# Softmax weights in ten chunks per head instead of twelve, and the pair gate and sums moved to GpSimd

## The reference

```python
def block(i):                       # 128 queries
    ...
    score = jnp.where(causal[None], score, -jnp.inf)
    _, sel = lax.top_k(score, topk)              # 256 keys
    logits = jnp.einsum('bqhd,bqkhd->bqhk', q_b, k_sel) * att_scale
    p = jax.nn.softmax(logits, axis=-1)
    return jnp.einsum('bqhk,bqkhd->bqhd', p, v_sel)
...
y_attn = group_rmsnorm(y_attn, gn_attn, N_HEADS) * jax.nn.silu(az)   # per head of 64
y = jnp.concatenate([y_conv, y_attn], axis=-1) @ w_out
return x + gate[:, None, :] * y
```

## Time and profile before

| | us |
|---|---|
| median of 3 runs | 722.95 (721.53 to 723.73) |
| the profiled execution's own time | 727.4 |
| its span, first to last instruction | 725.2 |
| PE busy | 673.8 (93%) |
| DVE busy | 468.8 (65%) |
| ACT busy | 372.0 (51%) |
| POOL busy | 220.4 (30%) |

### The profile page before, as it was taken

The page is one execution under the profiler, slowest core; times in us unless marked ns, Lnnn a source line. Parts: engine busy times, 40 slices in busy tenths (PEclk is TensorE's granted clock), DMA queues, the critical chain, the costliest instruction groups (busy, mean ns, idle before and its releaser), DMA issues.

```text
span 725.2 us, 8966 instructions
## 1 busy us (share of the span) xinstructions
PE 673.8 (93%) x3219; PEld 556.9 (77%) x3219; DVE 468.8 (65%) x772; ACT 372.0 (51%) x559; POOL 220.4 (30%) x109
## 2 busy tenths in 40 slices
PE   0889997999999999999999999998998999899996
...
GB/s 316 306 257 1 89 165 167 94 178 106 89 87 88 59 49 39 59 29 59 58 30 30 106 213 70 18 174 140 267 117 112 93 118 1 59 85 61 174 116 58
DMA packets 27910, 78.63 MB, mean 108 GB/s; under 512 B 3986, under 2 KB 8410, under 8 KB 27868
## 3 DMA queue, kind: packets, MB, share of 16 engines
...
q10 hardware_dynamic: 344, 1.05, 0.6%
...
## 4 chain that ended last, share of the span: by engine, by line
PE 77%; DVE 9%; ACT 4%; issue 4%; DMA 3%; SPq 2%; ACTq 1%; DVEq 0%
PE ps L726 15%; PE ps L728 15%; PE ps L727 15%; PE ps L906 4%; PE ps L907 4%; PE ps L908 4%; PE ps L844 4%; PE ps L784 2%; PE ps L785 2%; DMA iqs<-hlL 2%; PE ps L765 2%; PE ps L766 2%; DVE acc L1328 2%; DVE phL L1535 2%; PE ps L858 1%
## 5 line engine op out<-in xcount | busy, mean ns | idle before, releaser
L726 PE MATMUL ps<-hH,wH 128*128 128x512 f32 (+1 forms) x544 | 212.5, 391 | 1.5 <-issue 1.4
L728 PE MATMUL ps<-hH,wL 128*128 128x512 f32 (+1 forms) x544 | 211.0, 388 | 0.0
L727 PE MATMUL ps<-hL,wH 128*128 128x512 f32 (+1 forms) x544 | 211.0, 388 | 0.0
L1687 POOL TENSOR_TENSOR wL<-raw,wH 128x1024 fp32r<-128x1024 f32 x35 | 85.7, 2448 | 188.4 <-ACT wH L959 188.4
L726 PEld LDWEIGHTS ps<-hH,wH 128*128 128x128 f32 x544 | 102.6, 189 | 21.8 <-issue 3.2
L728 PEld LDWEIGHTS ps<-hH,wL 128*128 128x128 f32 x544 | 102.6, 189 | 20.5
L727 PEld LDWEIGHTS ps<-hL,wH 128*128 128x128 f32 x544 | 102.7, 189 | 18.4
L1527 DVE CUSTOM_DVE_ANT_0 ps<-ps,bias 128x128 f32<-128x128 f32 (+3 forms) x64 | 48.7, 761 | 45.7 <-PE ps L766 43.7
L1535 DVE TENSOR_TENSOR phL<-ps,phH 128x512 fp32r<-128x512 f32 (+1 forms) x96 | 52.6, 554 | 23.0 <-ACT phH L1164 17.4
L1144 ACT ACTIVATE relu<-ps,wabs 128x384 f32<-128x384 f32 (+5 forms) x48 | 40.2, 848 | 45.1 <-PE ps L785 24.6
L1421 DVE SCALAR_TENSOR_TENSOR score<-relu,wsgn,score 128x384 f32<-128x384 f32 (+5 forms) x42 | 49.7, 1184 | 19.2 <-ACT relu L1144 16.7
...
## 6 DMA issues: line engine op xcount, KB each, us to landing
raw<-in_w_units SPq DMA_DIRECT2D x36, 512.0 KB, 3.3
...
xin<-in_x SPq DMA_DIRECT2D x8, 512.0 KB, 7.9
wa<-in_w_ada SPq DMA_DIRECT2D x8, 512.0 KB, 11.8
...
gw<-in_w_ada SPq DMA_DIRECT2D x8, 512.0 KB, 3.7
...
wo<-in_w_out SPq DMA_DIRECT2D x8, 512.0 KB, 9.3
```

The costliest lines, as they stand in the source:

```text
L726: pe.matmul(out, wH[slot(n)][:, kt, :], hH[:, kt, cols], start=(kt == 0), stop=False)
L727: pe.matmul(out, wH[slot(n)][:, kt, :], hL[:, kt, cols], start=False, stop=False)
L728: mm = pe.matmul(out, wL[slot(n)][:, kt, :], hH[:, kt, cols], start=False, stop=(kt == KT - 1))
L1687: g.tensor_tensor(wL[slot(n)][:], raw[slot(n)][:], wH[slot(n)][:].bitcast(F32), ALU.subtract).then_inc(s_wL, 1)
```

## The change

**Chunks.** The chunks are now lists of key blocks. In half 0 the chunks of block 1 (384 columns) and block 3 (128) become one of 512 columns, (1, 3), block 3 in the free first 128 columns of the bank; in half 1 the same is done with blocks 5 and 7. A head has 3 + 7 = 10 chunks, of which eight are 512 columns wide and two 256. PE transposes and multiplies as much as before; `split_prob` and `low_prob` are 10 each instead of 12. The order within a half changes to 0, (1, 3), 2 and 0 to 4, (5, 7), 6. All tables are written anew for 20 half steps per head.

**Pair gate and sums.** `pair_gate` is now a product of `ya` and `azs` on POOL, and the gain goes into `pair_scale` on DVE at the end. As POOL has the sum not at hand in PSUM, ACT first copies it into `azs` (`keep_sums`, at x = 10 and 14), and POOL adds `dden` in place (`pair_add`). `keep_sums` waits for the sum (`s_yss`) and for POOL's gate product (`s_ygP`), since it writes over `azs`. PE's logits that reuse the banks now wait for `keep_sums` (`s_sums`) instead of `pair_add`. The last pair stays on DVE (`last_gate`, `last_add`, `last_scale`).

**Semaphores.** To make room for the new ones, the loads of the first two tiles of x share a semaphore (the first square waits for both), and so do two pairs of the loads of the last part of `w_ada`.

```diff
@@ -161,26 +161,26 @@
 NPH = 3
 PV_LAG = 2
 
-STEPS = 12
-LOGITS_AT = (4, 11, 13, 16, 18, 21, 23, 26)
-MAX_AT = (6, 11, 14, 16, 17, 22, 23, 25)
-EXP_AT = (10, 14, 17, 17, 22, 24, 27, 30)
+CHUNKS = ([(0,)] + [(1, 3)] + [(2,)], [(j,) for j in range(5)] + [(5, 7)] + [(6,)])
+STEPS = len(CHUNKS[0]) + len(CHUNKS[1])
+LOGITS_AT = (4, 9, 11, 14, 16, 18, 19, 22)
+MAX_AT = (5, 9, 12, 14, 15, 19, 19, 21)
+EXP_AT = (8, 12, 15, 15, 19, 20, 22, 24)
 FIRST_LOGITS = {2: 0, 3: 1, 4: 2, 5: 3, 6: 4, 10: 5, 12: 6, 14: 7}
 TMP_AT, OUT_AT = 4, 5
 LAST = 2 * STEPS * (NH - 1)
 
-DSQ_AT = {24 * (2 * t + 1) + (9 if t < NT - 1 else 7): t for t in range(NT)}
-DENS_AT = {24 * (2 * t + 1) + (11 if t < NT - 1 else 9): t for t in range(NT)}
-KEEP_AT = {24 * (2 * t + 1) + (13 if t < NT - 1 else 11): t for t in range(NT)}
-SUMS_AT = {24 * (2 * t + 2) + 11 + 4 * half: (t, half) for t in range(NT - 1) for half in range(2)}
-SUMS_AT[LAST + 17] = (NT - 1, 0)
-GATE_AT = {24 * (2 * t + 2) + 12: t for t in range(NT - 1)}
-ADD_AT = {24 * (2 * t + 2) + 13 + 4 * half: (t, half) for t in range(NT - 1) for half in range(2)}
-ADD_AT[LAST + 19] = (NT - 1, 0)
-OUT_HIGH_AT = {24 * (2 + ct) + 15: ct for ct in range(4)}
-OUT_HIGH_AT.update({LAST + x: 4 + n for n, x in enumerate((13, 16, 20, 22))})
-OUT_LOW_AT = {LAST + x: 4 + n for n, x in enumerate((15, 18, 22))}
-EARLY_PARTS = {4: 2, 5: 2, 6: 2, 7: 3, 8: 3, 10: 2, 11: 2}
+HEAD = 2 * STEPS
+DSQ_AT = {HEAD * (2 * t + 1) + (7 if t < NT - 1 else 5): t for t in range(NT)}
+DENS_AT = {HEAD * (2 * t + 1) + (11 if t < NT - 1 else 7): t for t in range(NT)}
+KEEP_AT = {HEAD * (2 * t + 1) + (13 if t < NT - 1 else 9): t for t in range(NT)}
+SUMS_AT = {HEAD * (2 * t + 2) + 9 + 4 * half: (t, half) for t in range(NT - 1) for half in range(2)}
+SUMS_AT[LAST + 15] = (NT - 1, 0)
+KEEP_SUMS_AT = {HEAD * (2 * t + 2) + 10 + 4 * half: (t, half) for t in range(NT - 1) for half in range(2)}
+OUT_HIGH_AT = {HEAD * (2 + ct) + 12: ct for ct in range(4)}
+OUT_HIGH_AT.update({LAST + x: 4 + n for n, x in enumerate((11, 14, 17, 18))})
+OUT_LOW_AT = {LAST + x: 4 + n for n, x in enumerate((13, 16, 18))}
+EARLY_PARTS = {3: 2, 4: 2, 5: 2, 6: 3, 7: 3, 8: 2, 9: 2}
 
 
 def places(at):
...
@@ -401,18 +401,29 @@
 
             return slice(HD * (h % 2), HD * (h % 2) + HD)
 
-        def chunks(sb):
-
-            return [(j, max(0, j - 4 * sb)) for j in range(4 * sb + 4)]
-
-
-
-        CH = [(h, sb, j, c) for h in range(NH) for sb in range(2) for j, c in chunks(sb)]
-        CH_AT = {u[:3]: n for n, u in enumerate(CH)}
+        CH = [(h, sb, js) for h in range(NH) for sb in range(2) for js in CHUNKS[sb]]
+        CH_AT = {(h, sb, j): n for n, (h, sb, js) in enumerate(CH) for j in js}
+
+        def all_up_to(h, sb, j):
+
+            return max(CH_AT[(h, sb, x)] for x in range(j + 1))
 
         def last_chunk(g):
 
-            return CH_AT[(g // 2, g % 2, 4 * (g % 2) + 3)]
+            return all_up_to(g // 2, g % 2, 4 * (g % 2) + 3)
+
+        def blocks_of(sb, j):
+
+            return range(max(0, j - 4 * sb), 4)
+
+        def place(js, sb, j):
+
+            return -P * blocks_of(sb, j).start if js.index(j) else 0
+
+        def width(k):
+
+            h, sb, js = CH[k]
+            return slice(0 if len(js) > 1 else P * blocks_of(sb, js[0]).start, HALF)
 
         TMPS = {2 * last_chunk(g) + 2 + TMP_AT: g for g in range(2 * NH - 1)}
         OUTS = {2 * last_chunk(g) + 2 + OUT_AT: g for g in range(2 * NH - 1)}
...
@@ -488,7 +503,7 @@
             sp.dma_start(posi[:], a["positions"].rearrange("o (b p) -> (o b) p", p=P)).then_inc(s_pos, 16)
             load(0)
             for t in range(NB):
-                sp.dma_start(xin[:, t, :], a["x"][0, P * t:P * t + P, :]).then_inc(s_x[t], 16)
+                sp.dma_start(xin[:, t, :], a["x"][0, P * t:P * t + P, :]).then_inc(s_x[max(0, t - 1)], 16)
 
             def load_part(g):
 
...
@@ -757,7 +773,7 @@
                 if h >= 2 and h % 2 == 0 and i == 5:
                     pe.wait_ge(s_dc, h // 2)
                 if h >= 3 and h % 2 == 1 and i in (4, 5):
-                    pe.wait_ge(s_add, h - 3 + i - 3)
+                    pe.wait_ge(s_sums, h - 3 + i - 3)
                 dst = logit_bank(u)
                 q = qs[h % 2][:, P * i:P * i + P]
                 for o in range(0, n, HALF):
@@ -835,28 +851,34 @@
 
             def turn(k):
 
-                h, sb, j, c = CH[k]
-                if j == 0:
+                h, sb, js = CH[k]
+                if js[0] == 0:
                     pe.wait_ge(s_exp, NB * h + 4 * sb + 4 if k else NB)
                 if k >= 2:
                     pe.wait_ge(s_pl, k - 1)
-                for b in range(c, 4):
-                    mm = pe.transpose(ps[:, 4 + k % 2, P * b:P * b + P], prob_of(sb, b)[:, P * j:P * j + P], identF[:])
+                for j in js:
+                    for b in blocks_of(sb, j):
+                        o = P * b + place(js, sb, j)
+                        mm = pe.transpose(ps[:, 4 + k % 2, o:o + P], prob_of(sb, b)[:, P * j:P * j + P], identF[:])
                 mm.then_inc(s_tp, 1)
 
             def values(k):
 
-                h, sb, j, c = CH[k]
+                h, sb, js = CH[k]
                 g = 2 * h + sb
                 pe.wait_ge(s_pl, k + 1)
                 if k == 0:
                     pe.wait_ge(s_vv, NT)
-                if j == 0 and g >= 2:
+                if js[0] == 0 and g >= 2:
                     pe.wait_ge(s_o, g - 1)
-                out = ps[:, 6 + sb, P * c:HALF]
-                pe.matmul(out, VV[:, j, h, :], phH[:, k % NPH, P * c:HALF], start=(j == 0), stop=False, skip_group_check=True)
-                pe.matmul(out, VV[:, j, h, :], phL[:, k % 2, P * c:HALF], start=False, stop=(j == 4 * sb + 3),
-                          skip_group_check=True).then_inc(s_pv, 1)
+                for j in js:
+                    cols = slice(P * blocks_of(sb, j).start, HALF)
+                    src = slice(cols.start + place(js, sb, j), cols.stop + place(js, sb, j))
+                    out = ps[:, 6 + sb, cols]
+                    pe.matmul(out, VV[:, j, h, :], phH[:, k % NPH, src], start=(j == 0), stop=False, skip_group_check=True)
+                    mm = pe.matmul(out, VV[:, j, h, :], phL[:, k % 2, src], start=False, stop=(k == last_chunk(g)),
+                                   skip_group_check=True)
+                mm.then_inc(s_pv, 1)
 
             def denominators(t):
 
...
@@ -1176,9 +1197,18 @@
 
                 return azs[:, t, :] if half is None else azs[:, t, HALF * half:HALF * half + HALF]
 
+            def keep_sums(t, half):
+
+                act.wait_ge(s_yss, 2 * t + half + 1)
+                act.wait_ge(s_ygP, t + 1)
+                A(pair_cols(t, half), ps[:, sums_bank(t, half), :], ACT.Copy).then_inc(s_sums, 1)
+
             def pair_log(t, half=None):
 
-                act.wait_ge(s_add, 2 * t + (half if half is not None else 1) + 1)
+                if t < NT - 1:
+                    act.wait_ge(s_addP, 2 * t + 2)
+                else:
+                    act.wait_ge(s_add, half + 1)
                 z = pair_cols(t, half)
                 A(z, z, ACT.Ln, scale=1.0 / HD).then_inc(s_yln, 1)
 
...
                         weights(u)
                     if x in TMPS:
                         other_half(TMPS[x])
+                    if x in KEEP_SUMS_AT:
+                        keep_sums(*KEEP_SUMS_AT[x])
                     if x in OUT_HIGH_AT:
                         out_high(OUT_HIGH_AT[x])
...
+            def pair_scale(t):
+
+                dve.wait_ge(s_yrs, t + 1)
+                dve.wait_ge(s_ygP, t + 1)
+                v.scalar_tensor_tensor(ya[:, t, :], ya[:, t, :], vec[:, V_GA + t:V_GA + t + 1], azs[:, t, :],
+                                       ALU.mult, ALU.mult).then_inc(s_ya, 1)
+
...
@@ -1761,16 +1798,28 @@
                 pool.wait_ge(s_woH, ct + 1)
                 g.tensor_tensor(hL[:, ct, :], wo[:, ct, :], wo_high(ct).bitcast(F32), ALU.subtract).then_inc(s_woL, 1)
 
-            pair_square(0, 0)
-            pair_square(0, 1)
-            out_low(0)
-            pair_square(1, 0)
-            out_low(1)
-            pair_square(1, 1)
-            out_low(2)
-            pair_square(2, 0)
-            out_low(3)
-            pair_square(2, 1)
+            def pair_gate(t):
+
+                pool.wait_ge(s_ysq, 2 * t + 2)
+                g.tensor_tensor(ya[:, t, :], ya[:, t, :], azs[:, t, :], ALU.mult).then_inc(s_ygP, 1)
+
+            def pair_add(t, half):
+
+                pool.wait_ge(s_sums, 2 * t + half + 1)
+                pool.wait_ge(s_din, 32 * (t + 1))
+                cols = slice(HALF * half, HALF * half + HALF)
+                g.tensor_tensor(azs[:, t, cols], azs[:, t, cols], dden[:, cols], ALU.add).then_inc(s_addP, 1)
+
+            for t in range(NT - 1):
+                pair_square(t, 0)
+                if t:
+                    out_low(2 * t - 1)
+                pair_square(t, 1)
+                pair_gate(t)
```

(41 more changed lines are left out.)

66 lines of the change are left out of this document (26 added, 40 removed).

## The result

The changed kernel takes 734.68 us (median of 6 runs, 732.41 to 739.25) against 723.10 for the kernel before beside it: ratio 1.0169 [1.0134, 1.0203]. The sign holds, and so does the mechanism in the pair heads; that the plain heads stay as they are doesn't, nor does the size: +11.6 us where I said +4.7, above the top of the range. The profiled execution of the kernel before (727.4 us) is slower than all six behind the 723.10 (721.46 to 726.21), so that what follows compares stretches at whole clock and not the two profiles' totals.

What follows compares the result with a forecast made beforehand. No engine was full; a chain of waits among PE, ACT and DVE through each head bounds the kernel. Terms 4.2 + 0 - 0.5 + 1.0 + 0 = +4.7 on 722.95 gave 727.6, stated as 727.5 us, range 719 to 731.5.

Steps and rivals of the forecast that it cites:

- The sign: Whole kernel: the change makes it slower, given a chance of 0.60 against 0.20 same and 0.20 faster.
- the mechanism in the pair heads: Pair heads: ACT stands 2.6 us at its first copy of the sums, waiting for POOL's product.
- Plain heads: Three plain heads between the first and the last: stay at 15.7 us each, change 0, between -0.4 and +0.3.
- The sixth logits' wait: Second piece of a head: sixth logits stand right behind an exponential on ACT, 0.1 to 0.4 us of waiting.
- The bound of +0.3: Plain heads: the most that one was expected to grow, in us, around a forecast change of 0.
- Pair heads: Three pair heads: about 18.6 us each, +1.4 each and +4.2 together, bounds -1.44 and +2.6 each.
- Softening 0.5: Pair heads: perhaps 0.5 us of ACT's stop comes back, since PE and DVE are at most two chunks behind.
- First head: Attention's first head: a 128-column chunk less in its first half saves 0.5 us, between -0.8 and 0.
- Last head: Last head: first output step waits +1.2 us, stop for the last pair's sum -0.2; together +1.0, between -0.5 and +2.5.
- Start: Kernel start: first square waiting for two tiles of x costs 0, at most +1.0; shared `w_ada` semaphores likewise.
- Stall absorbed: Rival, pair heads: idle 1.5 to 2 us of each head takes in the wait; 723.3 us, chance 0.22.
- Relief of DVE: Rival, all heads: work leaving DVE comes back whole, pair heads fall to plain ones; -6.6, 716.5 us, chance 0.17.

Runs made afterwards that it cites:

- e4: Changed kernel with one number changed: the maximum of block 5 at x = 18 instead of 19, ahead of a low part on DVE; 734.94 us, ratio 1.0145.
- e6: Changed kernel with ACT's closing `tmp` behind the split of the 256-column chunk instead of ahead of it; 734.97 us, ratio 1.0161.
- e1: Changed kernel's ten chunks, but gate and additions of pairs 0 to 2 back on DVE, no copies of sums on ACT; 735.62 us, ratio 1.0200.
- e8: Kernel before with its twelve chunks, pair gate and sums on POOL, ACT copies at x = 12 and 16, product in two halves; 719.86 us, ratio 0.9964.
- e3: Changed kernel with POOL's product in two halves, the first right behind the first half's square; 730.08 us, ratio 1.0111.
- e2: Kernel before with its twelve chunks, pair gate and sums on POOL, ACT's copies of sums at x = 12 and 16; 721.23 us, ratio 0.9975.

## Why the prediction was off

- **Plain heads, 0 predicted: the step that failed.** Measured +0.82, and it sits in all six heads (e4 shows 16.32 and 19.60, 3.28 apart, where 16.53 and 19.82 are 3.29): 4.9 us. I had read the places: "in its place ACT now does the closing `tmp` [...] and a 256-column chunk behind the last exponential". I then set its cost off against shed columns without following who waits for that low part (PE's second `turn`): 0.64 us in h1 (e6). The sixth logits' wait, priced at 0.1 to 0.4, was there and was 0.52, and the wait at the maximum of block 5, worth 0.22 (e4), I hadn't traced. The bound of +0.3 was too low because it rested on busy time, not on the order.
- **Pair heads, +1.4 each.** The mechanism was right: ACT's stop, released by POOL's product, at the predicted place. Over the plain head of its own kernel I took a pair head 2.9 longer; measured 3.29, 3.28 (h4 of e4) and 2.63. The parts too: stop 2.6 (2.70), head_out 1.4 after the `turn` (1.73), product's end 5.6 (6.0), ACT ready 3.0 (3.4). Softening 0.5 (2.70 cost 2.43: 0.3). Less before's own 1.46 a pair head, the sum is +4.8 for +4.2.
- **First head, -0.5.** At whole clock e1's first stretch took 18.50 us and e8's 18.88: -0.4.
- **Last head, +1.0.** 107.74 (changed, e3) against 105.34 and 105.42 (e2, e8): +2.4; before's 106.98 holds a fall of the clock. Its place was one step off: the denominators' 0.97, not the first output step itself, and the stop for the sum grew by 0.7 where I had it shrink by 0.2. PE's idle time ahead of the first output step is 0.97 + 0.37 = 1.3 us, at the lower end of my 1.3 to 2; with the stop for the sum these waits grew by 1.6 us together, and the rest of the 2.4 isn't traced.
- **Start, 0.** The first square begins at 9.38 us (9.71 before), and e2 and e8, which have the shared semaphores, are no slower than before.
- Together -0.4 + 4.9 + 4.8 + 2.4 = 11.7, measured 11.6 in the medians. That the match is so close is luck: the terms are those of whole clock, with e2's last stretch in place of before's, and what the clock cost in the median executions is not known. The two profiled spans differ by 8.0 only: up to the attention -3.7, first stretch +0.4, the six heads +10.6 (0.85 of it the clock in h3), last stretch +0.8. What doesn't depend on it is the heads' +9.7 where I had +4.2.

"Stall absorbed" was half true of another kernel: with twelve chunks and the copy at x = 12 the pair head stays at 17.28. "Relief of DVE" is refuted for this change, though e8 shows about 0.6 of its 1.44 us a pair head with the stop taken away: 16.6. The product was not slowed: 2.37 to 2.39 us, 1.87 times the 1.28 of DVE's gate, which is another instruction with one operand more. The Trainium skill, page "GPSIMD Engine Reference", section "Elementwise — side-by-side cycle accounting", measures GpSimd 1.96 times slower than DVE for a two-input add; the trace roughly agrees.
